# Scores of the windowed attention as stacked rounded products, and the modulation sums turned by 32 by 32 blocks

## The reference

```python
def swa_attention(q, k, v, sinks):          # 16 query heads of 64, 2 key heads
    ...
    scores = jnp.einsum('bnqhgd,bnkhd->bnhgqk', qb, kk).astype(jnp.float32) * (SWA_HEAD_DIM ** -0.5)
    ...
    probs = jax.nn.softmax(jnp.concatenate([scores, sink], axis=-1), axis=-1)[..., :-1]
    out = jnp.einsum('bnhgqk,bnkhd->bnqhgd', probs.astype(v.dtype), vv)

def modulation(cond, w, b, n):
    m = jax.nn.silu(cond) @ w[:, :n * D_MODEL] + b[:n * D_MODEL]
    return jnp.split(m, n, axis=-1)
```

## Time and profile before

| | us |
|---|---|
| three runs, median (lowest, highest) | 1671.52 (1669.97, 1673.87) |
| the profiled execution | 1672.03 |
| its span, first to last instruction | 1670.2 |
| TensorE busy in it | 1643.7 (98%) |
| VectorE busy | 1343.9 (80%) |
| ScalarE busy | 899.7 (54%) |

### The profile page before, as it was taken

How to read it: one execution, slowest core, us unless ns; L and a number is a source line. 1 busy time by engine, 2 the same in 40 slices (tenths; PEclk the granted TensorE clock), 3 DMA queues, 4 the chain that set the end, 5 groups by cost and what they waited for, 6 DMA issues and landing times.

```text
span 1670.2 us, 23384 instructions
## 1 busy us (share of the span) xinstructions
PE 1643.7 (98%) x8638; PEld 1400.1 (84%) x8638; DVE 1343.9 (80%) x1772; ACT 899.7 (54%) x1348; POOL 157.4 (9%) x221
## 2 busy tenths in 40 slices
PE   9999999999999999999999999999999999999996
PEld 8888888888888888887877878888877879999985
DVE  6998778979987878787985788888876988867766
ACT  6447564445466654565853466666534374445532
POOL 1100000001100000011211110010101101110000
PEclk9999999999999999999999999999999999999998
DMA  9975555658855545789987964345859869887663
GB/s 328 323 251 176 176 166 164 207 193 292 289 172 173 187 145 182 270 284 331 358 282 235 295 226 136 130 138 182 317 185 341 311 217 293 275 269 261 240 203 111
DMA packets 113160, 388.86 MB, mean 233 GB/s; under 512 B 18252, under 2 KB 19164, under 8 KB 111676
## 3 DMA queue, kind: packets, MB, share of 16 engines
q1 hardware_dynamic: 74944, 268.99, 45.9%
q0 software_dynamic: 27824, 101.18, 19.8%
q10 hardware_dynamic: 10286, 17.25, 3.0%
HBM read 383.19 MB, written 4.19 MB: 232 GB/s over the span
## 4 chain that ended last, share of the span: by engine, by line
PE 93%; DVE 3%; DMA 2%; ACT 1%; issue 1%; DVEq 0%; ACTq 0%; SPq 0%
PE L L396 22%; PE L L397 22%; PE L L403 22%; PE L L442 4%; PE L L438 4%; PE L L436 4%; PE TP L534 3%; PE AB L2601 2%; PE AB L2301 1%; DMA stage<-in_w_stream 1%; PE TP L2314 1%; PE AB L2535 1%; PE AB L2617 1%; PE AB L2304 1%; PE AB L2327 1%
## 5 line engine op out<-in xcount | busy, mean ns | idle before, releaser
L317 ACT ACTIVATE wh<-stage 128x1024 fp32r<-128x1024 f32 x504 | 530.4, 1057 | 463.8 <-PE L L403 221.9
L338 DVE TENSOR_TENSOR wl<-stage,wh 128x1024 fp32r<-128x1024 f32 x504 | 612.8, 1221 | 203.3 <-ACT wh L317 201.8
L396 PE MATMUL L<-wh,xth 128*128 128x512 f32 (+1 forms) x1692 | 680.9, 402 | 1.9 <-DVE xtl L2026 1.3
L397 PE MATMUL L<-wh,xtl 128*128 128x512 f32 (+1 forms) x1692 | 659.0, 389 | 0.0
L403 PE MATMUL L<-wl,xth 128*128 128x512 f32 (+1 forms) x1692 | 454.0, 389 | 0.0
L396 PEld LDWEIGHTS L<-wh,xth 128*128 128x128 f32 x1692 | 318.2, 188 | 67.1 <-issue 3.2
L403 PEld LDWEIGHTS L<-wl,xth 128*128 128x128 f32 x1692 | 317.5, 188 | 66.4 <-DVE wl L338 1.0
L397 PEld LDWEIGHTS L<-wh,xtl 128*128 128x128 f32 x1692 | 318.5, 188 | 62.7 <-issue 2.4
L714 DVE SCALAR_TENSOR_TENSOR macc<-mstage,scols,macc 128x1024 f32<-128x1024 f32 x240 | 306.8, 1278 | 4.3 <-DMA mstage<-in_w_mod 3.8
L781 POOL DMA_DIRECT2D mstage<-in_w_mod x192 | 138.9, 724 | 1240.7 <-DVE macc L714 1044.5
L436 PE MATMUL L<-xth,wh 128*128 128x256 f32 x512 | 125.8, 284 | 0.0
(11 more groups left out here) (275 smaller groups left out, 1464.5 us busy)
## 6 DMA issues: line engine op xcount, KB each, us to landing
stage<-in_w_stream SPq DMA_DIRECT2D x504, 512.0 KB, 4.6
mstage<-in_w_mod POOLq DMA_DIRECT2D x192, 512.0 KB, 6.2
arena<-in_ctx ACTq DMA_DIRECT2D x1, 2048.0 KB, 9.2
x_kept<-X ACTq DMA_DIRECT2D x4, 512.0 KB, 10.3
X<-x_kept ACTq DMA_DIRECT2D x1, 2048.0 KB, 8.3
arena<-in_b_ada ACTq DMA_DIRECT2D x2, 1024.0 KB, 9.1
arena<-in_ln_g ACTq DMA_DIRECT2D x2, 1024.0 KB, 8.8
X<-in_x SPq DMA_DIRECT2D x3, 512.0 KB, 8.1
```

Source lines behind the costliest of these rows:

```text
L317: nc.scalar.activation(wh[:, s % SPLITS].rearrange("p a b -> p (a b)"), stage[:, s % RING, :], ACT.Copy).then_inc(hi_ready, 1)
L338: nc.vector.tensor_tensor(wl[:, s % SPLITS].rearrange("p a b -> p (a b)"), stage[:, s % RING, :], wh[:, s % SPLITS].rearrange("p a b -> p ...
L396: nc.tensor.matmul(dst[:, t, 0:width], xh, w, start=start and k == 0, stop=False, skip_group_check=True)
L397: nc.tensor.matmul(dst[:, t, 0:width], xl, w, start=False, stop=False, skip_group_check=True)
```

## The change

Scores. ScalarE now copies each turned group of queries, scaled, in the rounded format (`queries_high`), into the 64 partitions of its key group; VectorE writes the remainder into the other 64 (`queries_low`). The keys are stored rounded in both halves (`keys_hi`, by ScalarE) and their remainder in one half with zeros in the other (`keys_lo`, by VectorE). A score is then q * keys_hi + q * keys_lo, both in the rounded format, four products for a head instead of two float32 ones. The stacked tiles lie in `heads`, over the last third of the arena.

Sums. `mod_turn` turns `macc` in place by blocks of 32 x 32 on VectorE, `mod_part` sums the 1024 columns to 32 per partition, and TensorE adds over the four groups of partitions with one small product (`turn_sums`, 128 x 32), which takes one turn instead of two. VectorE then picks out the columns with four small copies (`mod_columns`). In a layer the first two of these products now follow the scores in heads 2 and 3; three steps of `mod()` that stood before the heads are moved, one to head 0, one to head 2 and one into the later loop over the other eight heads. In the context part the second product moves next to the third.

```diff
 def layer_turns(l):
-    t += [("k", l, 0), ("qa", l, 0)] + [("m", l, 0, w, j) for w in range(2) for j in range(2)]
-    t += [("qa", l, c) for c in range(1, 4)] + [("lat", l, i) for i in range(3)]
-    t += [("t", l, h) for h in range(AH - 1)] + [("ya", l, 0), ("t", l, AH - 1), ("ya", l, 1), ("ya", l, 2)]
+    t += [("k", l, 0)] + [("qa", l, c) for c in range(4)] + [("lat", l, i) for i in range(3)]
+    for h in range(AH - 1):
+        t += [("t", l, h)] + ([("m", l, 0, h - 2)] if h in (2, 3) else [])
+    t += [("ya", l, 0), ("t", l, AH - 1), ("ya", l, 1), ("ya", l, 2)]
...
+        def mod_turn(dve, l, i, w):
+            dve.wait_ge(mod_sum, mod_done(l, i + 1))
+            nc.vector.transpose(macc[:, w, :], macc[:, w, :]).then_inc(once("sums_turned"), 1)
+        def mod_part(dve, n, w):
+            dve.wait_ge(once("sums_turned"), n)
+            nc.vector.tensor_reduce(part[:, n % 2, :], macc[:, w, :].rearrange("p (n j) -> p n j", j=32), AX.X, ALU.add)\
+                .then_inc(once("part_ready"), 1)
...
-            for j, m in enumerate(turns):
-                dve.wait_ge(tp_ready, m)
-                nc.vector.tensor_reduce(msum[:, 4 * j:4 * j + 4], TP[(m - 1) % 2].rearrange("p a (c n) -> p (a c) n", n=P),
-                                        AX.X, ALU.add).then_inc(bank_free(m), 1)
+            dve.wait_ge(tp_ready, m)
+            for a in range(4):
+                rows = slice(32 * a, 32 * a + 32)
+                ins = nc.vector.tensor_copy(msum[rows, :], TP[(m - 1) % 2][rows, 0, a:32:4])
+            ins.then_inc(bank_free(m), 1)
...
+                def queries_high(c):
+                    m = TURN["qa", l, c]
+                    act.wait_ge(tp_ready, m)
+                    for g in range(2):
+                        ins = nc.scalar.activation(queries[g][HALF[g], 2 * c:2 * c + 2, :], TP[(m - 1) % 2][HALF[g], :, :], ACT.Copy,
+                                                   scale=AD ** -0.5)
+                    ins.then_inc(once("queries_high"), 1)
...
+                def queries_low(c):
+                    m = TURN["qa", l, c]
+                    dve.wait_ge(once("queries_high"), 4 * l + c + 1)
+                    for g in range(2):
+                        q = queries[g][:, 2 * c:2 * c + 2, :]
+                        ins = nc.vector.scalar_tensor_tensor(out=q[HALF[1 - g]], in0=TP[(m - 1) % 2][HALF[g], :, :], scalar=AD ** -0.5,
+                                                             in1=q[HALF[g]].bitcast(F32), op0=ALU.mult, op1=ALU.subtract)
+                    ins.then_inc(bank_free(m), 1)
...
-                    mod()
+                    if h in (3, 4):
+                        mod_unit(0, h - 3)
+                    mod(2 if h in (0, 2) else 1)
...
+            def turn_sums(n, m):
+                pe.wait_ge(once("every32"), 4)
+                pe.wait_ge(once("part_ready"), n)
+                turned(pe, m - 2)
+                nc.tensor.matmul(TP[(m - 1) % 2][:, 0, 0:32], every32[:].rearrange("p a i -> p (a i)"), part[:, n % 2, :], start=True,
+                                 stop=True).then_inc(tp_ready, 1)
...
-                            last = nc.tensor.matmul(AB[b][:, o], qaT[:, h % 8, qs], kaT[:, h // 8, keys], start=True, stop=True)
+                            q = queries[h // 8][:, h % 8, qs]
+                            nc.tensor.matmul(AB[b][:, o], q, keys_hi[:, h // 8, keys], start=True, stop=False)
+                            last = nc.tensor.matmul(AB[b][:, o], q, keys_lo[:, h // 8, keys], start=False, stop=True)
...
+                    if h in (2, 3):
+                        turn_unit(0, h - 2)
                     step(GA + 9 + 2 * h)
```

More of the change, by code:

```diff
@@ L163, in build @@
         ones_r = sb("ones_r", [P, P], F32R)
+        every32 = sb("every32", [P, 4, 32])
+        part = sb("part", [P, 2, 32])
         L = [ps(f"L{b}", [P, TT, COLS]) for b in range(2)]
@@ L184, in build @@
         TB = 12288
-        qaT, kaT = ar(TB, 8, TOK), ar(TB + 2048, 2, TOK)
+        queries = [heads[:, 8 * g:8 * g + 8, :] for g in range(2)]
+        keys_hi, keys_lo = heads[:, 16:18, :], heads[:, 18:20, :]
+        HALF = [slice(0, 64), slice(64, 128)]
         qnT, knT = ar(TB, 4, TOK), ar(TB + 1024, 4, TOK)
@@ L723, in mod_columns_from, with mod_columns @@
                                            op0=ALU.add, op1=ALU.add).then_inc(mod_cols, 1)
-        def mod_columns(dve, n, w, turns, which, layer, c, scale):
+        def mod_turn(dve, l, i, w):
[5 more added lines that the diff above has]
+                .then_inc(once("part_ready"), 1)
+        def mod_columns(dve, n, w, m, which, layer, c, scale):
             if MOD_COLS[n] + w:
                 dve.wait_ge(mod_cols, MOD_COLS[n] + w)
-            for j, m in enumerate(turns):
-                dve.wait_ge(tp_ready, m)
-                nc.vector.tensor_reduce(msum[:, 4 * j:4 * j + 4], TP[(m - 1) % 2].rearrange("p a (c n) -> p (a c) n", n=P),
-                                        AX.X, ALU.add).then_inc(bank_free(m), 1)
-            for m in turns:
-                turned(dve, m)
+            dve.wait_ge(tp_ready, m)
[3 more added lines that the diff above has]
+            ins.then_inc(bank_free(m), 1)
+            turned(dve, m)
             mod_columns_from(msum, which, layer, c, scale)
@@ L897, in attention_layer @@
                               + [(PROJ[:, t, 0:256], ss2[:, 2 + t:3 + t], 256) for t in range(TT)], e0 + 1, JUNK)
-                hi(5)
+                hi()
+                m = TURN["k", l, 0]
+                act.wait_ge(tp_ready, m)
+                for g in range(2):
+                    for rows in HALF:
+                        ins = nc.scalar.activation(keys_hi[rows, g, :], TP[(m - 1) % 2][HALF[g], 0, :], ACT.Copy)
+                for g in range(2):
+                    ins = nc.scalar.activation(krT[HALF[g], g, :], TP[(m - 1) % 2][HALF[g], 1, :], ACT.Copy)
+                ins.then_inc(once("keys_high"), 1)
+                queries_high(0)
+                hi(3)
+                queries_high(1)
+                queries_high(2)
+                hi()
+                queries_high(3)
                 for i, (a, n) in enumerate(LAT_KT):
@@ L1391, in copy_turned @@
                 if name[0] == "k":
[L1392 to L1397, removed]
+                    dve.wait_ge(once("keys_high"), name[1] + 1)
+                    for half, p in enumerate(HALF):
+                        ins = nc.vector.tensor_tensor(keys_lo[p, half, :], bank[p, 0, :], keys_hi[p, half, :].bitcast(F32), ALU.subtract)
                 else:
@@ L1411, in mod_unit @@
                 def mod_unit(i, w):
-                    mod_columns(dve, 2 * l + i, w, [TURN["m", l, i, w, j] for j in range(2)], 1 - w, 0, 8 * l + KT * i, i == 1)
+                    mod_columns(dve, 2 * l + i, w, TURN["m", l, i, w], 1 - w, 0, 8 * l + KT * i, i == 1)
                 def rope_k():
@@ L1506, in attention_layer @@
                         lo()
+                    dve.wait_ge(ident_loaded, 16)
+                    nc.vector.tensor_reduce(every32[:, 0, :], ident[:].rearrange("p (a i) -> p i a", a=4), AX.X, ALU.add)\
+                        .then_inc(once("every32"), 1)
+                    dve.wait_ge(once("every32"), 1)
+                    for a in range(1, 4):
+                        nc.vector.tensor_copy(every32[:, a, :], every32[:, 0, :]).then_inc(once("every32"), 1)
                     dve.wait_ge(silu_c, 1)
@@ L2361, in turn_unit @@
                 def turn_unit(i, w):
-                    turn_sums(l, i, w, [TURN["m", l, i, w, j] for j in range(2)])
+                    turn_sums(4 * l + 2 * i + w + 1, TURN["m", l, i, w])
                 step(GA + 2)
-                turn_unit(0, 0)
                 step(GA + 3)
-                turn_unit(0, 1)
                 step(GA + 4)
```

74 lines of the change are left out of this document (39 added, 35 removed).

## The result

The changed kernel takes 1679.26 us (median of 14 runs, 1675.43 to 1683.81) where the kernel before took 1671.82 on the same chips: a ratio of 1.0038, 95% interval 1.003 to 1.0046. The prediction was 1669.1, with a range of 1664 to 1676: the forecast of a gain was 10.2 us too low, and the time lies 3.3 us above the range. The profiled execution is 1679.39 us, its span 1677.6, at a mean granted clock of 0.992 (0.997 before).

A forecast was written before the change was run, and what follows sets the result against it. TensorE, busy 1643.7 of 1670.2 us, was taken to bound the kernel. Two layers (-1.1) and the context part (-1.3) gave -2.4 us on the profiled 1672.03, 1669.6; the median lies 0.5 lower, so 1669.1, range 1664 to 1676.

The forecast's parts named there:

- The scores: TensorE's four rounded products take 0.53 us a head instead of 0.72, some 0.22 saved, 7.0 us for 32 heads.
- Rival 2: Narrow rounded score products cost as much as float32 ones, 0.21 us; nearly nothing saved there, total 1673.7; chance 0.13.
- The sums: On TensorE one small product, 0.29 us with changeover, replaces a sum of 0.88: 0.59 saved, 6.5 us for 11 sums.
- the rival of a dear block turn: Block turn costs its upper bound, 1.8 us, or waits before the heads are 3 us; total 1671.5; chance 0.14.
- Before the heads: TensorE waits about 1.0 us for turns and head 0's scores (bounds 0 and 4), reaching head 0 about 0.9 earlier.
- The wait in head 3: Second adding product waits 4.3 us for bank TP1, which VectorE frees late; a layer is 3.05 us later through head 3.
- rival 1: Clock falls in the wait of head 3, 2.0 us or up to twice that lost behind each; total 1674.1; chance 0.18.
- the step moved to head 2: Second modulation step in head 2, taken at 1.2 us, makes VectorE's slot remainder ahead of the head 3 wait later.
- The prediction's own sign of failure: The prediction as a whole fails if TensorE waits for something in the heads behind head 4.
- The context part: Three sums save 1.8 us, 0.5 lost to VectorE's added block turns and sums (bounds 0 and 2.4): -1.3.

The follow-up runs named there:

- e1_early: Changed kernel with VectorE's copies of the first added sum one head earlier (heads 2 and 3 instead of 3 and 4): 1668.04 us, ratio 0.997.
- e8_order: Changed kernel with first-sum copies one head earlier, a modulation step moved to head 5, one block turn and one sum put behind the query remainders: 1663.63 us.
- e2_warm: Changed kernel with 20 unread float32 products on TensorE in front of the second adding product of each layer: 1672.31 us, ratio 1.0001.
- e3_mods: Changed kernel with one modulation step per layer moved from the later loop (m = 4) to head 5 of the first: 1677.34 us, ratio 1.0031.
- the two parts alone: Kernel before with only the sums part, 1678.8 us (ratio 1.0034), and with only the scores part, 1670.83 us (ratio 0.9986).

## Why the prediction was wrong

**The scores: right.** Steps of 0.15, 0.11, 0.17 and 0.12 us, 0.55 for a head where I had 0.53; slot starts fall by 0.22 a head from 169 to 231 us and again in layer 1 (2.4 each time, as summed). Rival 2 falls: the narrow rounded product takes 0.11 to 0.15, and a float32 product of 128 columns 4.54/20 = 0.227.

**The sums: right.** 0.9 us go with each sum ahead of the heads, two late ones give 1.2. The adding product takes 0.14 us in front of the next slot (`e1_early`) where 0.29 was taken. By form, the block turn, the sum behind it and the query remainders:

```profile
L735 DVE STREAM_TRANSPOSE macc<-macc 128x1024 f32<-128x1024 f32 x11 | 13.6, 1236 | 0.0
L740 DVE TENSOR_REDUCE part<-macc 128x32 f32<-128x1024 f32 x11 | 13.3, 1212 | 0.1
L1514 DVE SCALAR_TENSOR_TENSOR heads<-TP,heads 64x512 fp32r<-64x512 f32 x16 | 11.0, 688 | 0.8 <-ACT heads L871 0.5
```

1.24, 1.21 and 0.69 for 1.2, 1.3 and 0.68; so the rival of a dear block turn falls too.

**Before the heads: mis-sized.** I had 1.0 us of waits and head 0 reached 0.9 earlier. The waits are 0.16, 0.77 and 0.48, 1.4 a layer, and cost 1.9 by the slot starts, as much as the two sums had saved: head 0 comes at the time of before in both layers. 1.8 us of the miss. `e8_order` shows the cause, a block turn and a sum in the way of the remainders, for 1.3 of the 1.9.

**The wait in head 3: right in place, cause and length.** The copies began at 152.0 where I had their end at 151.9, but TensorE came later as well, so the wait was 4.39 for 4.3. From head 0 to behind the wait the kernel without the clock's share (`e2_warm`) loses 4.2 us for 3.95: 0.5 of the miss in both layers.

**The clock: the step that failed.** The sum of the forecast has no term for a fall of the clock behind the wait in head 3. The prediction had the mechanism only as its rival 1, at 0.18, with a price of 2.0 to 4 us a wait; it measured 2.35 and 2.0, 4.35 of the miss, and both falls came in each of the two traces that have waits of 4.4 us (in `e3_mods` they cost 2.6 and 2.7). Without these 4.35 the time would have been 1674.9, inside the range. What failed is the weighing. I set one wait of 3.55 us without a fall against a wait longer than that, and against the fall at the end of the same kernel, which came within 2 us of the last product. A single wait is a sample and not a limit: in the ten traces the clock fell in 7 of 8 waits of 3.2 us and more (that of before is the eighth), in 8 of 15 of 2.1 to 2.5 us, and in none that was shorter. The wait near 977 is 2.26 us in all ten, and the clock fell there in five. That the trace of the kernel before shows no fall seems to be chance: the three traces without a fall ahead of the end have a mean granted clock of 0.997 over the span, the others 0.996 or less, and of the 51 later executions of the kernel before, 37 are at 0.996 or less. By that measure it falls in most executions of that kernel too. The rule that the prediction named beside this rival (the Trainium skill, TensorE: Matmul & The Clock Gate, Part 1: throttled is the default, and only activity releases it) agrees with these traces, 0.50 behind idle stretches of 2.1 to 4.4 us and 1.00 again after 3 to 6 us of products.

**A modulation step: left out.** The prediction counted the step moved to head 2 but not the one that takes its way to m = 4 of the later heads. It makes scores late by 0.9 and slots by 1.1, 2.2 us in the two layers. The prediction's own sign of failure ("if TensorE waits for something in the heads behind head 4") is this wait.

**The context part: right in itself, and lost behind it.** From 699 to 934 us the slots go from +7.5 to +5.4, about 0.7 for each of the three sums, where -1.3 was forecast; none of the 0.5 that it set aside for VectorE's added work shows in the slot starts. The wait at 794 is 1.1 us shorter than before, but the clock's fall at its end takes that back. What the prediction had no term for lies behind: 1.6 for the fall at 977 us, behind a wait as long as before, and 0.9 at 1301, less 0.4 in small steps. From 699 us to the end that is -0.1, 1.2 of the miss. Both places are one trace's: falls at 977 came in half of the traces, and the wait near 790 moves by itself: 3.55, 2.49, 3.24, 0.56 and 1.3 us in the traces of the kernel before, the changed one, `e1_early`, `e2_warm` and `e3_mods`, of which the last three alter nothing near it.

Sum of the misses: 1.8 + 0.5 + 4.35 + 2.2 + 1.2 = 10.05, less 0.3 that the changed kernel was ahead at 40 us, 9.75; forecast -2.4, measured +7.4, 9.8. This sum is one of two traces; that the medians too differ by 7.4 is partly luck, since both kernels have falls and waits that other executions don't show.

What stays open: what decides whether the clock falls in an idle stretch of 2 to 3.6 us, how much of the 7.4 us between the medians of `e2_warm` and of the changed kernel lies outside the two filled waits, why the two parts alone are 4.4 us from their sum, and what moves the wait near 790.

## What to carry to other kernels

An instruction that TensorE issues in order and that waits for a far end of another engine's list costs its wait and half as much again: here 4.4 us of waiting and 2 to 2.7 us for half clock behind it. Before moving a step, look at which instruction frees its bank and where in that engine's list it stands, and put the freeing right behind what it needs (one line here, 11.7 us). Where a step is moved off a place at which the old order had a gap, look at what the gap made room for. And when one example stands against a mechanism, and the same trace shows the mechanism at another place, price it into the forecast and not into a rival; the mean granted clock of several executions tells whether the one that was traced is typical.

## What the runs showed of the hardware

- Work that nobody reads keeps the clock: 20 products into a free bank in front of each of the two waits kept it at 1.00, and the kernel was 7.4 us faster (4.35 of it traced to the clock behind these waits), although the adding product came no earlier.
- Idle stretches of 2.14 and 2.15 us in one execution ended with the clock at 1.00 and at half, and behind one of 2.26 us at the same place of the program it fell in five of ten traces; the length of the wait alone doesn't decide. The Trainium skill (TensorE: Matmul & The Clock Gate, Part 1) says that the chip looks at activity at times that run free of the kernel, so that one kernel meets another phase in each execution; these waits agree with that, though no run here varied the phase alone.
- The clock can fall when the engine is busy again: at 977 us TensorE resumed at 978.96, and it fell about 1.3 us later.
- A stretch at half clock outlasts the wait: in the changed kernel the clock was back about 5 us after TensorE resumed at 152.8. So a short wait in which it falls costs nearly as much clock as one twice as long: 1.6 us behind 2.26, 1.8 behind 3.54, 2.0 and 2.35 behind 4.4.
